# Layer 1 of the first block rebuilt: projections by tokens without a norm, paired fp32r scores, cross-attention first

## The reference, cut to what matters

```python
h = rms_norm(x, norm_mix[1])
q, k, v, f_logit, xq = split(h @ w_in, [512, 1024, 1536, 1544])
q = rms_norm(heads(q), q_gain); k = rms_norm(heads(k), k_gain)   # 8 heads of 64
c = cumsum(log_sigmoid(f_logit + b_f), axis=1)
s = (q @ k.T) / 8 + c[query] - c[key];  s = where(query >= key, s, -1e30)
y_mix = softmax(s) @ v
# 4 heads of 128, into 256 memory tokens
y_mem = softmax(rms_norm(xq) @ rms_norm(mem_k).T / sqrt(128)) @ mem_v
x = x + concat([y_mix, y_mem]) @ w_out
x = x + square(relu(rms_norm(x, norm_mlp) @ w1)) @ w2            # 4096 hidden
```

## Time and profile before

| | us |
|---|---|
| median of 3 runs | 3056.34 (3054.72 to 3065.91) |
| profiled execution | 3049.57 |
| its span | 3048.1 |
| PE / DVE / ACT / POOL busy | 2858.8 / 1680.4 / 992.1 / 195.1 |
| chain that ended last, by engine | PE 85%, DVE 9%, ACT 3%, issue 3%, POOL 1% |
| mean granted TensorE clock | 0.958 of full speed |

### The profile page before, as it was taken

How to read it: one execution, slowest core, us unless ns; L and a number is a source line. 1 busy time by engine, 2 the same in 40 slices (tenths; PEclk the granted TensorE clock), 3 DMA queues, 4 the chain that set the end, 5 groups by cost and what they waited for, 6 DMA issues and landing times.

```text
span 3048.1 us, 45161 instructions
## 1 busy us (share of the span) xinstructions
PE 2858.8 (94%) x18925; PEld 2347.3 (77%) x18925; DVE 1680.4 (55%) x2280; ACT 992.1 (33%) x1323; POOL 195.1 (6%) x246
## 2 busy tenths in 40 slices
PE   6979999979799999998999989999889999899997
PEld 6768888868578888787878768888678878688886
DVE  6667777767658777646434443333575343533334
ACT  5533222224442222242333332223433332332222
POOL 3100000000000000002030000000020030000000
PEclk8989999979899999899999999999999999899998
DMA  4214555412025555221003322232210023222221
GB/s 156 78 63 135 179 169 172 152 42 83 2 70 156 169 165 169 92 87 38 3 29 101 97 83 97 96 97 84 77 56 11 3 69 97 83 97 97 96 93 59
DMA packets 239085, 282.15 MB, mean 93 GB/s; under 512 B 7492, under 2 KB 225928, under 8 KB 238920
## 3 DMA queue, kind: packets, MB, share of 16 engines
q1 hardware_dynamic: 225598, 227.48, 23.5%
q0 software_dynamic: 12960, 52.14, 5.8%
q10 hardware_dynamic: 362, 0.11, 0.0%
HBM read 277.58 MB, written 2.10 MB: 92 GB/s over the span
## 4 chain that ended last, share of the span: by engine, by line
PE 85%; DVE 9%; ACT 3%; issue 3%; POOL 1%; DVEq 0%; ACTq 0%; POOLq 0%
PE psum L1987 23%; PE psum L1988 23%; PE psum L1989 23%; DVE wlo L1289 1%; PE psum L2049 1%; PE psum L2342 1%; PE psum L2328 1%; ACT whi L763 1%; PE psum L2312 1%; DVE rest L1303 1%; PE psum L2264 1%; DVE rest L1308 1%; PE psum L2278 1%; PE psum L2136 1%; DVE rest L1320 0%
## 5 line engine op out<-in xcount | busy, mean ns | idle before, releaser
L1987 PE MATMUL psum<-hh,whi 128*128 128x512 f32 x2112 | 838.6, 397 | 38.6 <-DVE hl L1327 19.8
L1988 PE MATMUL psum<-hl,whi 128*128 128x512 f32 x2112 | 831.3, 394 | 0.0
L1989 PE MATMUL psum<-hh,wlo 128*128 128x512 f32 x2112 | 830.6, 393 | 0.0
L1289 DVE TENSOR_TENSOR wlo<-raw,whi 128x2048 fp32r<-128x2048 f32 x224 | 522.6, 2333 | 537.8 <-ACT whi L763 537.0
L763 ACT ACTIVATE whi<-raw 128x2048 fp32r<-128x2048 f32 x224 | 427.6, 1909 | 585.2 <-PE psum L1989 556.1
L1987 PEld LDWEIGHTS psum<-hh,whi 128*128 128x128 f32 x2112 | 402.7, 191 | 135.4 <-issue 34.8
L1987 PE MATMUL psum<-mh,whi 128*128 128x512 f32 (+1 forms) x1184 | 458.8, 388 | 19.3 <-DVE ml L1461 8.2
L1988 PEld LDWEIGHTS psum<-hl,whi 128*128 128x128 f32 x2112 | 402.7, 191 | 84.6 <-issue 1.7
L1989 PEld LDWEIGHTS psum<-hh,wlo 128*128 128x128 f32 x2112 | 402.0, 190 | 85.2
L1988 PE MATMUL psum<-ml,whi 128*128 128x512 f32 (+1 forms) x1184 | 456.6, 386 | 0.0
L1989 PE MATMUL psum<-mh,wlo 128*128 128x512 f32 (+1 forms) x1184 | 456.5, 386 | 0.0
(11 more groups left out here) (361 smaller groups left out, 2821.2 us busy)
## 6 DMA issues: line engine op xcount, KB each, us to landing
rest<-in_ada_w POOLq DMA_DIRECT2D x64, 768.0 KB, 5.3
raw<-in_w_gu SPq DMA_DIRECT2D x44, 1024.0 KB, 5.0
raw<-in_w_in SPq DMA_DIRECT2D x34, 1024.0 KB, 5.3
raw<-in_w_mlp_in SPq DMA_DIRECT2D x32, 1024.0 KB, 5.6
raw<-in_w_mlp_out SPq DMA_DIRECT2D x32, 1024.0 KB, 5.2
raw<-in_w_out SPq DMA_DIRECT2D x16, 1024.0 KB, 5.2
raw<-in_w_down SPq DMA_DIRECT2D x16, 1024.0 KB, 5.1
raw<-in_w_mem_kv SPq DMA_DIRECT2D x8, 1024.0 KB, 5.3
```

What stands on the lines that cost most here:

```text
L1289: dve.tensor_tensor(wlo[:, g % 2, :, :], raw[:, g % 2, :, :], f32(whi[:, g % 2, :, :]), ALU.subtract)\
L1987: pe.matmul(out, whi_, xhi, start=first, stop=False)
L1988: pe.matmul(out, whi_, xlo, start=False, stop=False)
L1989: return pe.matmul(out, wlo_, xhi, start=False, stop=last)
```

## The change

- `norm_mix` of layer 1 becomes a raw norm: the operand tiles are x times gain, made beside the last MLP chunk of layer 0 (which is taken out of the loop, in both layers), and the token factor (`tk`, one number per token) is applied to the products.
- v, k and q are projected by tokens. Slabs are stored 264 columns wide; v's second slab brings the 8 forget logits. The order is v1, v0, k0, k1, xq0, xq1, q0, q1. The head factors of q and k are made by tokens: ACT squares, DVE reduces over 64 features, ACT root, DVE reciprocal and product (`token_heads`). Then q and k are turned by PE (16 transposes each) and split into high and low fp32r parts (`kh`, `kl`, `qh`, `ql`).
- adaLN's 48 columns are issued among the matmuls of v0. Head means of the queries of both cross-attentions become single columns (`query_sums`) beside `gate` slab 1 and q0; their factor goes into the scale of the exponential, both gains into the memory keys.
- The decay is summed on PE by a triangular matrix (`cum`), over softplus values on 128 partitions x 32; POOL's two DMAs and the `f` slab go.
- Cross-attention comes ahead of fox attention, with the turn of q after its third unit. Fox attention goes through 16 units of two heads x 128 queries: three fp32r products a head, each head on one half of PE's rows, the decay as a product with -1, the mask in fp32r; values of the two heads in the two column halves of one bank.
- `wo` of layer 1 takes operand tiles 4 to 7 first. POOL makes two more constants, DVE rounds five to fp32r.

```diff
-RAW_NORMS = (1, 3)
+RAW_NORMS = (1, 2, 3)
...
+    def attend_pairs(self, l):
+        for j in range(PAIRS + 3):
+            if j < PAIRS:
+                self.pair("fox_s", l, j)
+            if 2 <= j < PAIRS + 2:
+                self.pair("fox_t", l, j - 2)
+            if j >= 3:
+                self.add("fox_o", l, j - 3)
...
+                self.slab_jobs("v", 1, 1, NT)
+                self.add("ms", 2)
+                self.slab_jobs("v", 1, 0, NT)
                 self.add("mod", 0)
-                self.lin("f", l, 1, 1)
-                self.mixed("xq", l, 2, 2, "hn", 1, 0)
-                self.mixed("q", l, 2, 2, "hn", 1, 4)
-                self.mixed("k", l, 2, 2, "hn", 1, 8)
-                self.mixed("v", l, 2, 4, "hn", 1, 12)
-                self.attend("fox", l, 4 * FOX_H)
+                self.slab_jobs("k", 1, 0, NT)
+                for i in range(4):
+                    self.add("hn", 1, i)
+                self.slab_jobs("k", 1, 1, NT)
+                self.slab_jobs("xq", 1, 0, 2)
+                for t in range(4):
+                    self.add("kT", t)
+                self.slab_jobs("xq", 1, 1, 2)
+                self.add("cum", 0)
+                self.slab_jobs("q", 1, 0, NT)
+                self.add("xs", 1)
+                self.slab_jobs("q", 1, 1, NT)
             self.attend("xa", l, 2 * XA_H)
+            if l:
+                self.attend_pairs(l)
...
-        raw = sb("raw", [P, 2, KT, SLAB])
-        whi = sb("whi", [P, 2, KT, SLAB], F32R)
-        wlo = sb("wlo", [P, 2, KT, SLAB], F32R)
+        raw = sb("raw", [P, 2, KT, WIDE])
+        whi = sb("whi", [P, 2, KT, WIDE], F32R)
+        wlo = sb("wlo", [P, 2, KT, WIDE], F32R)
...
+            q.step(pool.memset(tri, 1.0))
+            q.step(pool.affine_select(out=tri, in_=tri, compare_op=ALU.is_ge, fill=0.0, base=0,
+                                      pattern=[[1, P]], channel_multiplier=-1))
+            q.step(pool.memset(pick, 0.0))
+            for i in range(4):
+                q.step(pool.affine_select(out=pick, in_=pick, compare_op=ALU.not_equal, fill=-1.0, base=-32 * i,
+                                          pattern=[[-1, FOX_H]], channel_multiplier=1))
...
+                    def token_heads(name, s, x):
+
+                        for b in range(NT + 1):
+                            if b < NT:
+                                j, n = J[name, l, s, b], NT * x + b
+                                ready(act, j)
+                                if n >= 2:
+                                    act.wait_ge(S("head_sum"), n - 1)
+                                act.activation(sq_tok[:, n % 2, :], bank(j)[:, 0:SLAB], ACT.Square).then_inc(S("token_sq"), 1)
+                            if b:
+                                n, c = NT * x + b - 1, 8 * (b - 1) + 4 * s
+                                act.wait_ge(S("head_sum"), n + 1)
+                                act.activation(hn[:, 0, c:c + 4], hn[:, 0, c:c + 4], ACT.Sqrt, scale=1.0 / HD,
+                                               bias=tk[:, 2, b - 1:b]).then_inc(S("head_root"), 1)
...
-                    for t in range(2):
-                        head_norm(x_sq, 0, 4, t, x_tiles(t))
...
-                    head_norm(x_sq, 0, 4, 2, x_tiles(2))
+                    query_factors()
...
+                    evacuated(dve, J["ms", 2])
+                    dve.reciprocal(tk[:, 1, :], tk[:, 0, :]).then_inc(S("token_factor"), 1)
+                    dve.scalar_tensor_tensor(tk[:, 2, :], tk[:, 0, :], EPS, tk[:, 0, :], ALU.mult, ALU.mult)\
+                       .then_inc(S("token_factor"), 1)
+                    lo(slab_of("v", 0))
...
+                    lo(slab_of("k", 1))
+                    token_heads("k", 0, 0, kn)
+                    adaln(0)
+                    for t in range(4):
+                        head_norm(m_rs1, l, 0, t, mem_tiles(t), MEM)
+                    lo(slab_of("xq", 0))
+                    token_heads("k", 1, 1, kn)
+                    lo(slab_of("xq", 1))
+                    lo(slab_of("q", 0))
+                    turned("kT", 0, kh, kl, V("fox_k_gain"))
...
+                        if l == 0 and cc == CHUNKS1 - 1 and i >= 5:
+                            raw_lo(2, lambda t: V("norm_mix", 8 + t), (2 * i - 10, 2 * i - 9))
+                            norm_sums(2, range(max(1, 2 * i - 10), 2 * i - 8))
...
-                    linear("f", l, 0, h, before=normed(2), blocks=1)
-                    means = [mean_128, mean_128, mean_64, mean_64]
-                    for g, name in enumerate(("xq", "q", "k", "v")):
                         for s in range(2):
-                            if name == "v":
-                                linear_tokens("v", l, s, h, NT)
-                            else:
-                                linear(name, l, s, h)
-                            if s == 0:
-                                head_means(l, 4 * g, means[g], h_sq, T if g else MEM)
...
-                        pe.matmul(p[:, 0:n], qaug[0:a, hd, t * P:(t + 1) * P], kaug[0:a, hd, 0:n], start=True, stop=False)
-                        return pe.matmul(p[:, t * P:n], ident[:, :], causal[:, :], start=False, stop=True)
...
+                    linear_tokens("v", l, 1, h, NT, n=WIDE, before=normed(2))
+                    pe.wait_ge(S("norm_added"), 7 * 2 + 7)
+                    p = start("ms", 2)
+                    for b in range(NT):
+                        ins = pe.matmul(p[:, b:b + 1], n_acc[:, b * P:(b + 1) * P], mean_all[:, 0:1], start=True, stop=True)
+                    done(ins)
+
+                    mods = bank(J["mod", 0])
+
+                    def adaln_beside(b, k):
+
+                        if (b, k) == (1, 0):
+                            ahead("mod", 0)
+                            pe.wait_ge(ada_done, 256 + 16)
+                        for n in range(16 * b + 2 * k - 16, 16 * b + 2 * k - 14) if b else ():
+                            ins = pe.matmul(mods[:, n:n + 1], ada_acc[:, n * P:(n + 1) * P], ones[:, 0:1], start=True, stop=True)
+                        return ins if b else None
+                    linear_tokens("v", l, 0, h, NT, beside=adaln_beside)
+                    start("mod", 0)
+                    done(pe.matmul(mods[:, 47:48], ada_acc[:, 47 * P:48 * P], ones[:, 0:1], start=True, stop=True))
+                    linear_tokens("k", l, 0, h, NT)
+                    head_means(1, 0, mean_128, m_sq1, MEM)
+                    linear_tokens("k", l, 1, h, NT)
...
+                    linear("xq", l, 0, h)
+                    turned("kT", kn, "k")
+                    linear("xq", l, 1, h)
+                    p = start("cum", 0)
+                    pe.wait_ge(S("log_forget"), 1)
...
+                    linear_tokens("q", l, 0, h, NT, beside=sums_beside)
+                    start("xs", 1)
+                    done(query_sums(1, sums, x_sq1, NT - 1, XA_H - 1))
+                    linear_tokens("q", l, 1, h, NT)
+                    half = [slice(0, HD), slice(HD, P)]
+
+                    def fox_scores(j):
+
+                        h, t = j // NT, j % NT
+                        n, o = P * (t + 1), slice(t * P, (t + 1) * P)
+                        p = [start("fox_s", l, j, i) for i in range(2)]
+                        for left, right, first in ((qh, kh, True), (ql, kh, False), (qh, kl, False)):
+                            for i in range(2):
+                                a = half[i]
+                                pe.matmul(p[i][:, 0:n], left[a, h, o], right[a, h, 0:n],
+                                          start=first, stop=False)
+                        for i in range(2):
+                            a = slice(HD * i, HD * i + 32 + FOX_H)
+                            pe.matmul(p[i][:, 0:n], minus[a, 2 * h + i:2 * h + i + 1].to_broadcast([32 + FOX_H, P]),
+                                      cr[a, 0:n], start=False, stop=False)
+                        for i in range(2):
+                            done(pe.matmul(p[i][:, t * P:n], unit[:, :], later[:, :], start=False, stop=True))
+
+                    def fox_turn(j, i):
+
+                        p = start("fox_t", l, j, i)
+                        pe.wait_ge(S("fox_probs"), 2 * j + i + 1)
+                        for k in range(j % NT + 1):
+                            ins = pe.transpose(p[:, k * P:(k + 1) * P], f_p[:, (2 * j + i) % 6, k * P:(k + 1) * P], ident[:, :])
+                        done(ins)
+
+                    def fox_values(j):
+
+                        h, t = j // NT, j % NT
+                        p = start("fox_o", l, j)
+                        for i in range(2):
+                            evacuated(pe, J["fox_t", l, j, i])
                         for k in range(t + 1):
+                            for i in range(2):
+                                c = (2 * h + i) * HD
+                                ins = pe.matmul(p[half[i], 0:P], vtok[:, k, c:c + HD], f_a[:, (2 * j + i) % 4, k * P:(k + 1) * P],
```

(12 more changed lines are left out.)

528 lines of the change are left out of this document (352 added, 176 removed).

## The result

Before 3055.5 us (median, 3054.5 to 3065.9), after **3039.0 us** (3033.5 to 3042.3): a ratio of 0.993, 95% interval [0.991, 0.995]. The forecast was 2993 us with a range of 2976 to 3019. The kernel is faster, as forecast, but by 16.5 us instead of 63, and outside the range. The profiled execution's span is 3040.7 us against 3048.1.

The account below looks back on a forecast made before the run. TensorE, busy 94% of the span, was taken as the bound. Layer 1's mixer 198 us against 261.2 (-63.2), prologue +2.7 and layer 0 -2.2 gave -62.7 from 3056.3: 2993 us, range 2976 to 3019 (eight in ten).

Parts of the forecast that it names:

- prologue: Start of the kernel: seven more POOL steps and five small DVE copies behind the same wait, +2.7 us.
- v slab 0 with adaLN's 49 columns, with cold clock: Layer 1's projections: 11.5 us for the slab, 10.7 for columns at 0.109 each, 1.5 for cold clock.
- xa: Layer 1's cross-attention, now first: 23.9 us becomes 27.7 with table load and q transposes; range 25 to 31.
- fox (and 3 for handovers): Layer 1's forgetting attention: 50 us against 70.9, at 2.8 a pair, plus 3 for handovers not followed.
- layer 0 beyond the prologue: Layer 0: -2.6 us by earlier scans, less 0.4 for a second table load: -2.2 us.
- slab rows now lie 264 apart: nothing, see the last rival: Slab buffers: the wider row spacing was costed at nothing.
- rival C: Matmuls of 512 columns read rows 1056 bytes apart; 6.3 ns more pitch loses all, 10 ns gives 3092 us; chance 0.02.
- four head means become 17 columns: nothing: Layer 0: head means of 3.43 us become single columns of 3.7 us, costed at nothing.
- `lo` ends at 174.2, scans at 178.7: Layer 0: two head norms leave the chain, so scans end at 178.7 instead of 181.3 us, -2.6 us.
- Rival A: Fox attention keeps its 70 us: halves don't overlap, tile changes drain, or lower clock; +20, 3013 us; chance 0.22.
- Rival B: Layer 1's projections hang on DVE and ACT, with late low parts and cold clock; 3006 us; chance 0.13.
- xq's `lo`: Layer 1's projections: about 11 us of DVE work covered by 11.5 us of k slab 1; without cover up to 2 us.

Follow-up runs that it names:

- b_wide: Kernel before the change with only the three slab buffers widened to 264 columns, rows 1056 bytes apart instead of 1024: 3094 us, ratio 1.012.
- a_near: Changed kernel with rows of 1024 bytes in all slabs but the 264 wide one, and 192 unused bytes ahead of hh: 3000 us, ratio 0.982.
- b_all64: Kernel before the change with 64 unused bytes ahead of the slab buffers, so weights and moving tiles all move together: 3069 us, one run.

## Why the prediction was wrong, and where it was right

| step | forecast | changed kernel |
|---|---|---|
| prologue | +2.7 | +2.8 |
| v slab 1 to 264 columns | 12.0 | 11.7 |
| stop for v slab 0's low part | 3.4 | 2.8 |
| v slab 0 with adaLN's 49 columns, with cold clock | 23.7 | 24.4 |
| k, xq, transposes, decay, q | 77.3 | 76.9 |
| projections in all | 117.3 | 116.7 (628.3 to 745.0) |
| xa | 27.7 | 29.9 |
| fox (and 3 for handovers) | 53 | 47.8 |
| layer 0 beyond the prologue | -2.2 | +6.9 |
| **pitch of the 128x512 matmuls** | **0** | **+4.8 ns, 45 us** |

**The step that failed** is the one put as "slab rows now lie 264 apart: nothing, see the last rival", and its mechanism is rival C's, to which I gave 0.02. Its reason against, that weights and moving tiles are read in row pieces of 128 floats before and after, was an argument about the form of a read; the traces had no row at any other distance than 0 modulo 256, so it bounded nothing. I also priced the rival only from where it decides the sign (6.3 ns) and gave 10 ns as its example. At 4.8 ns it costs 45 us without turning the sign, and the range had no room for that. b_wide shows it by itself (+4.9 ns in the kernel before), a_near takes it away.

With the pitch back (a_near) the first block ends as forecast: PE waits for the second block's first norm sum at 1210.53 us, where the kernel before has 1272.35, 61.8 us earlier against a forecast of 62.7. That this is so near is in part luck: prologue and layer 0 came 4.4 us too late (4.9 against 0.5), the mixer 2.7 better (65.9 against 63.2, fox 5 better and xa 2 worse), the MLP of layer 0 1.0 better. Its median is 3000, 56.9 under the kernel before beside it, with 2993 forecast. The rest is not settled: in the profiled a_near the second block, which is the same in both, took 12.5 us more than in the profiled execution before (1777.6 against 1765.1), with the granted clock lower in several of its stages (0.93 against 0.97 in one, with nothing else to tell them apart), and that execution of before was itself 6.8 under its median. b_all64, whose pitch and program are those of before, took 3069 in its one run.

**Layer 0** was mis-sized by 9 us: -2.2 forecast, +6.9 measured. Two steps failed, and neither by the price of its instructions.

The step "four head means become 17 columns: nothing" had the columns right. At full clock four of them between two tiles of gate slab 1 cost 0.45 us, 0.113 each, so 3.8 for the 34 against 3.7. It left out what the head means had hidden, though I had asked of other edits what hides them: the stop of 2.07 us, and the 1.6 us at the lower clock behind it. Slab 1 takes 16.57 us (122.92 to 139.49) in the changed kernel and 14.96 (121.33 to 136.29) in a_near.

The step "`lo` ends at 174.2, scans at 178.7" was right as far as it went. In a_near, whose stretch starts 6.03 us later than before (168.22 against 162.19), they end at 174.5 and 179.0 in the old kernel's time. But of the 2.6 us only 0.9 reached PE there (first transpose at 193.05, 187.88 before), and nothing did in the changed kernel (197.25, with the stretch 9.25 later). Before, ACT's table load was done in the shadow of the low part; now it stands between the first maximum and the first exponential. The same row before and after:

```profile
175.86 1.28 ACT L835 ACT_TABLE_LOAD   x1
```

```profile
193.84 1.28 ACT L882 ACT_TABLE_LOAD   x1 [7.59 <-DVE stat L1513]
```

In the changed kernel the low part itself came 1 us later still, behind a slab that ran longer at the lower clock (granted 0.78 from 171.44 to 185.70; 0.87 before, 0.85 in a_near). a_near takes 4.6 of the 6.9 us away (184.4 against 189.0): up to 1.4 by the pitch of the 288 matmuls of 512 columns, about 1.5 by the clock in gate slab 1, 0.9 by the clock in this slab, the rest in smaller differences. Why the clock differs between the two is not shown.

**Cross-attention** took 29.9 us where 27.7 were forecast. Its exponentials now read their scale from a tensor, which the prediction priced at nothing: one of 128x256 takes 0.56 us instead of 0.47, and a unit's cycle 3.25 instead of 3.08, 1.4 us over the eight.

**Rival A** (fox keeps its pace, 70 us) is refuted: 47.8 us, with the changes of tile size inside it. **Rival B** is refuted: no stop over 2.8 us in the projections. The cover of "xq's `lo`" by k slab 1 held. In v slab 0 the one-column matmuls cost 0.112 us each at full clock, where 0.109 was taken from two-column ones. The slab's other extra, 1.5 us at the lower clock (645.25 to 648.78, matmuls 0.213 apart instead of 0.119), came as forecast too. The 0.025 by the Trainium skill's price per matmul ("TensorEngine Tiling (Array Packing)", Instruction Overhead) stays refuted here.

## What to carry to other kernels

Widening a buffer or adding a small tensor ahead of TensorE's operands is an edit of its own: count the pitch of the unchanged matmuls in one full-clock window of both traces before you look for a lost gain among the waits, because a page with PE at 94% shows nothing of it. In this kernel keeping the distance from the stationary tile to the moving tile a multiple of 256 bytes, row by row, was worth 45 us by count times pitch, and 39 between the medians of the changed kernel and a_near (3039.0 and 2999.9); when something forces a wider row, lay out only that buffer so. And a rival that is priced only at the point where it turns the sign leaves out all its values below: give an operation that no row bounds its own spread in the range. When you take work away that stood ahead of a wait, price the wait that it hid and what a stop does to the clock behind it.

## What the runs showed of the hardware that I had not expected

- The pitch of a 128x512 matmul with split operands at full clock: 226.7 ns at a distance of 0 modulo 256 bytes, 228.9 at 64, 232.4 at 128, 233.3 at 32 and at 192, both between 400 and 480 us and between 1900 and 1980. The 256-column matmuls of the token slabs, where the slab is the moving operand, did the opposite, and less of it: from the first start to the last, 96 of them took 11.39 us at 0 and 11.19 at 192.
- DVE's low part of a slab (two inputs, 128x2048) takes 2.29 us alone and 5.94 beside a POOL product. By the Trainium skill, "SBUF — State Buffer", Who interferes with whom, a DVE instruction with two SBUF inputs contends with a GpSimd instruction that reads SBUF; this trace agrees, and in both cases shown above the DVE instruction, which started 0.83 and 0.54 us behind POOL's, ended only behind it, by 2.15 and 0.01 us.
- A pause of PE can cost a second time behind its end: after 2.07 us the next six matmuls ran 0.43 us apart instead of 0.23, at 1.2 GHz, and it cost 1.6 us more; after 2.30 us in a_near they did not.
- Two fp32r products in row halves run side by side, 0.133 us each with 512 columns, in whichever order the heads are issued.
